# Hybrid stages: values products half a slot later, a preloaded mask under the decay rows, and wider Exp instructions

## The reference, cut to what matters

```
def hybrid_mixer(h, w_in, ...):
    proj = h @ w_in
    q, k, v, z, xbc, dt = split(proj)
    attn = dilated_attention(rotary(q), rotary(k), v)      # 8 heads of 64
    xbc = silu(causal_depthwise_conv(xbc)); xs, bm, cm = split(xbc)
    dt = softplus(dt + dt_bias)
    y = ssd_chunked(xs, dt, -exp(a_log), bm, cm) + d_skip * xs
    return concat([attn, groupnorm(y * silu(z))]) @ w_out
def segsum_exp(a):                                          # in ssd_chunked, per chunk of 128 and head (16)
    cs = cumsum(a)
    return exp(where(lower_triangle, cs[:, None] - cs[None, :], -inf))
```

## Time and profile before

| what | value |
|---|---|
| times of three runs | 2692.08, 2696.5, 2701.61 us; median 2696.5 |
| span of the profiled execution (first to last instruction) | 2693.9 us, the only time that the page gives for it |
| PE busy | 2601.8 us, 97% of the span |
| DVE, ACT, POOL busy | 1815.6 us (67%), 1467.9 us (54%), 173.1 us (6%) |
| chain that ended last, by engine | PE 83%, DVE 7%, ACT 5% |
| mean granted TensorE clock | 0.993 |

### The profile page before, as it was taken

How to read it: one execution, slowest core, us unless ns; L and a number is a source line. 1 busy time by engine, 2 the same in 40 slices (tenths; PEclk the granted TensorE clock), 3 DMA queues, 4 the chain that set the end, 5 groups by cost and what they waited for, 6 DMA issues and landing times.

```text
span 2693.9 us, 44003 instructions
## 1 busy us (share of the span) xinstructions
PE 2601.8 (97%) x15456; PEld 2255.8 (84%) x15456; DVE 1815.6 (67%) x2565; ACT 1467.9 (54%) x2363; POOL 173.1 (6%) x253
## 2 busy tenths in 40 slices
PE   7999998999999989999989999999999999998999
PEld 6888887888888868888888688888888888887887
DVE  5766668666766666676676666676657667666766
ACT  4645447455555564565555655555555555555654
POOL 0010001000000030000001200000110000002000
PEclk9999999999999999999999999999999999999999
DMA  4458744477566436666654266666446665653664
GB/s 150 145 164 231 210 129 142 156 226 212 172 193 190 133 121 208 191 184 193 187 176 153 70 199 191 177 192 191 141 149 183 196 202 168 192 157 121 180 189 146
DMA packets 581774, 465.44 MB, mean 173 GB/s; under 512 B 19524, under 2 KB 542372, under 8 KB 581156
## 3 DMA queue, kind: packets, MB, share of 16 engines
q1 hardware_dynamic: 579300, 456.10, 56.3%
q0 software_dynamic: 1632, 7.37, 1.1%
q10 hardware_dynamic: 736, 0.56, 0.1%
HBM read 460.76 MB, written 4.25 MB: 173 GB/s over the span
## 4 chain that ended last, share of the span: by engine, by line
PE 83%; DVE 7%; ACT 5%; issue 2%; DVEq 2%; DMA 1%; POOL 1%; SPq 0%; ACTq 0%; POOLq 0%
PE acc L783 19%; PE gu L750 14%; PE tp L750 13%; PE tp L757 7%; PE gu L757 7%; PE acc L816 3%; DVE lo_a L452 3%; ACT hi_a L440 1%; PE acc L1454 1%; PE acc L1456 1%; PE acc L1455 1%; PE gu L701 1%; PE gu L1412 1%; PE tp L1327 1%; PE gu L1413 1%
## 5 line engine op out<-in xcount | busy, mean ns | idle before, releaser
L452 DVE TENSOR_TENSOR lo_a<-raw_a,hi_a 128x2048 fp32r<-128x2048 f32 (+1 forms) x313 | 711.1, 2272 | 357.4 <-ACT hi_a L440 356.1
L440 ACT ACTIVATE hi_a<-raw_a 128x2048 fp32r<-128x2048 f32 (+1 forms) x313 | 591.5, 1890 | 119.0 <-PE acc L1456 27.4
L750 PE MATMUL tp<-xT,hi_a 128*128 128x512 f32 x1600 | 398.4, 391 | 0.0
L750 PE MATMUL gu<-xT,hi_a 128*128 128x512 f32 x1600 | 397.9, 391 | 0.0
L750 PEld LDWEIGHTS gu<-xT,hi_a 128*128 128x128 f32 x1600 | 294.0, 188 | 56.9
L750 PEld LDWEIGHTS tp<-xT,hi_a 128*128 128x128 f32 x1600 | 293.4, 188 | 56.4
L783 PE MATMUL acc<-hi_b,h_hi 128*128 128x512 f32 x760 | 298.6, 393 | 1.6 <-issue 1.1
L783 PE MATMUL acc<-lo_b,h_hi 128*128 128x512 f32 x760 | 298.0, 392 | 0.0
L783 PE MATMUL acc<-hi_b,h_lo 128*128 128x512 f32 x760 | 295.7, 389 | 0.0
L464 DVE TENSOR_TENSOR lo_b<-raw_b,hi_b 128x1024 fp32r<-128x1024 f32 x210 | 255.9, 1219 | 0.0
L842 ACT ACTIVATE arena<-arena 128x256 f32<-128x256 f32 x200 | 83.6, 418 | 282.0 <-DVE arena L905 282.0
(11 more groups left out here) (329 smaller groups left out, 4109.4 us busy)
## 6 DMA issues: line engine op xcount, KB each, us to landing
raw_a<-in_ffn_w_in SPq DMA_DIRECT2D x352, 512.0 KB, 5.7
raw_b<-in_ffn_w_out SPq DMA_DIRECT2D x176, 512.0 KB, 3.6
raw_a<-in_w_in SPq DMA_DIRECT2D x52, 512.0 KB, 4.7
raw_a<-in_w_gate SPq DMA_DIRECT2D x44, 512.0 KB, 5.5
raw_a<-in_w_up SPq DMA_DIRECT2D x44, 512.0 KB, 6.7
raw_b<-in_w_down SPq DMA_DIRECT2D x44, 512.0 KB, 4.4
raw_a<-in_w_out SPq DMA_DIRECT2D x24, 512.0 KB, 4.2
raw_a<-in_c_w_in SPq DMA_DIRECT2D x24, 512.0 KB, 4.5
```

The source lines that it names most:

```text
L440: nc.scalar.activation(a_view(hi_a, par)[:, :, 0:width], a_view(raw_a, par)[:, :, 0:width], ACT.Copy).then_inc(a_hi, 1)
L452: nc.vector.tensor_tensor(a_view(lo_a, par)[:, :, 0:width], a_view(raw_a, par)[:, :, 0:width], a_view(hi_a, par)[:, :, 0:width].bitcast(F3 ...
L750: nc.tensor.matmul(banks[:, e, :], w_hi[:, kt, e * P:(e + 1) * P], xT[:, :, kt, :], start=(kt == 0), stop=False)
```

## The change

1. Values products of the hybrids run four half slots after the scores (before: three), and write PSUM bank `acc[:, 2, 0:256]` (before: a part of `tp`). The transposes no longer wait for `o_lo`; the values products do instead, that of unit 0 for `cs_out`. ScalarE's copy comes at the end of its half slot, after the hi split; VectorE's part half a slot after that.
2. At `p` = 11 VectorE runs `softplus_sum_dve` before the lo split (before: after it).
3. The triangular mask is loaded by two SP DMAs of 1 MB each into `mTs` ahead of slot 4's load (`masks_sync`); GpSimd's DMA adds the decay rows onto it (`accum_op`), in one run of 8 KB per partition (before: 512 B). VectorE adds the per-partition values (`segments_dve`, `p` = 15 and 17) in place of the mask. ScalarE runs Exp over eight heads at a time without bias, four instructions (before: 32), at `p` = 17 and 19.
4. ScalarE preloads, at `p` = 9, a table set that has both Exp and Ln.
5. `bc_pe` waits for `o_lo` of unit 3 in place of `cs_out`.

```diff
@@ mixer_sync
+                if s.kind == "hybrid" and i == 4:
+                    masks_sync(sp, s)
                 if n >= 2:
                     sp.wait_ge(a_lo, n - 1)
...
+        def masks_sync(sp, s):
+            if s.k == 0:
+                sp.wait_ge(bias_row_ready, 1)
+            else:
+                for t in range(NT):
+                    sp.wait_ge(x_ready[t], 2 * s.k)
+            lo, hi = CC["negtri"]
+            for c in range(NT):
+                sp.dma_start(mTs[c], T["constants"][:, lo:hi].unsqueeze(1).broadcast_to([P, SSM_HEADS, P])).then_inc(mask_in, 16)
@@ decay_pool
+            pool.wait_ge(mask_in, 32 * (L + 1))
             for c in range(NT):
-                pool.dma_start(mTs[c], decay_rows[L, c].partition_broadcast(P)).then_inc(row_in[c], 16)
+                src = decay_rows[L, c].rearrange("h l -> (h l)").partition_broadcast(P)
+                pool.dma_start(mTs[c].rearrange("p h l -> p (h l)"), src, accum_op=ALU.add).then_inc(row_in[c], 16)
@@ woven_turn_pe
-            elif w >= 1:
+            elif w >= 1 and s.kind != "hybrid":
                 pe.wait_ge(o_lo, s.pair0 + w)
@@ woven_values_pe
             pe.wait_ge(pt_act, g + 1)
+            if s.kind == "hybrid":
+                pe.wait_ge(*((o_lo, s.pair0 + w) if w else (cs_out, s.layer + 1)))
@@ middle_pe
-            if scored(s, p - 3) is not None and s.kind != "B":
-                woven_values_pe(pe, s, scored(s, p - 3))
+            behind = p - (4 if s.kind == "hybrid" else 3)
+            if scored(s, behind) is not None and s.kind != "B":
+                woven_values_pe(pe, s, scored(s, behind))
@@ bc_pe
-            pe.wait_ge(cs_out, L + 1)
...
+            pe.wait_ge(o_lo, s.pair0 + 4)
@@ hybrid_act
                     if p == 9:
+                        nc.scalar.preload_act_table_set("natural_log_exp_and_others")
                         narrow_evac_act(act, s, 3, dt_out)
...
-                    if scored(s, p - 3) is not None:
-                        values_act(act, s, scored(s, p - 3))
...
-                    if 15 <= p < 19:
-                        decay_act(act, s, (p - 15) // 2, 2 * ((p - 15) % 2))
+                    if p in (17, 19):
+                        decay_act(act, s, (p - 17) // 2)
...
                     if h == 0:
                         ahead_a(hi_slot_a, act, s.a0 + i + 1)
+                    if scored(s, p - 4) is not None:
+                        values_act(act, s, scored(s, p - 4))
@@ decay_act
+            for g in range(SSM_GROUPS):
+                m = mTs[c][:, 8 * g:8 * g + 8, :]
+                nc.scalar.activation(m, m, ACT.Exp).then_inc(seg_exp, 1)
@@ hybrid_dve
+                    if p == 11:
+                        softplus_sum_dve(dve, s)
                     if h == 1:
                         ahead_a(lo_slot_a, dve, s.a0 + i + 1)
...
-                    if scored(s, p - 3) is not None:
-                        values_dve(dve, s, scored(s, p - 3))
+                    if scored(s, p - 5) is not None:
+                        values_dve(dve, s, scored(s, p - 5))
...
-                    if p in (14, 16):
-                        causal_dve(dve, s, (p - 14) // 2)
+                    if p in (15, 17):
+                        segments_dve(dve, s, (p - 15) // 2)
@@ segments_dve (was causal_dve)
-            nc.vector.tensor_tensor(mTs[c], mTs[c], C("negtri").unsqueeze(1).broadcast_to([P, SSM_HEADS, P]), ALU.add)\
+            nc.vector.tensor_tensor(mTs[c], mTs[c], ncs[:, 16 * c:16 * c + 16].unsqueeze(2).broadcast_to([P, SSM_HEADS, P]), ALU.add)\
```

More of the change, by code:

```diff
@@ L359, in build_block @@
         row_in = [sem("row_in0"), sem("row_in1")]
+        mask_in = sem("mask_in")
         cs_ps, cs_out, decays, xdec_ready = sem("cs_ps"), sem("cs_out"), sem("decays"), sem("xdec_ready")
@@ L1255, in build_block, with values_bank @@
         turn_flat = tp[:, :, :].rearrange("p b c -> p (b c)")[:, 0:768]
+        def values_bank(s):
+            return acc[:, 2, 0:256] if s.kind == "hybrid" else tp[:, 1, 256:512]
         def score_banks(s, w):
@@ L1326, in woven_values_pe @@
                         cols_t = slice(512 + hh * P, 512 + (hh + 1) * P) if t else slice(hh * 256, (hh + 1) * 256)
-                        mm = nc.tensor.matmul(tp[r, 1, 256 + t * P:512], v[:, t, c:c + HD], probs_t[:, cols_t],
+                        mm = nc.tensor.matmul(values_bank(s)[r, t * P:256], v[:, t, c:c + HD], probs_t[:, cols_t],
                                               start=(j == pair[0] and t == 0), stop=(t == 1 and s.kind != "B"))
@@ L1506, in values_act @@
             act.wait_ge(o_ready, s.pair0 + u + 1)
-            nc.scalar.activation(oT_hi[:, u, :], tp[:, 1, 256:512], ACT.Copy).then_inc(o_hi, 1)
+            nc.scalar.activation(oT_hi[:, u, :], values_bank(s), ACT.Copy).then_inc(o_hi, 1)
         def exp_act(act, s, w):
@@ L1548, in values_dve @@
             dve.wait_ge(o_hi, s.pair0 + u + 1)
-            nc.vector.tensor_tensor(oT_lo[:, u, :], tp[:, 1, 256:512], oT_hi[:, u, :].bitcast(F32),
+            nc.vector.tensor_tensor(oT_lo[:, u, :], values_bank(s), oT_hi[:, u, :].bitcast(F32),
                                     ALU.subtract).then_inc(o_lo, 1)
@@ L2108, in silu_act, with decay_act @@
             nc.scalar.activation(conv[:, 2 * r:2 * r + 2, :], conv[:, 2 * r:2 * r + 2, :], ACT.Silu).then_inc(silued, 1)
[L2110 to L2116, removed]
+        def decay_act(act, s, c):
+            act.wait_ge(seg_ready, 2 * s.layer + c + 1)
+            for g in range(SSM_GROUPS):
+                m = mTs[c][:, 8 * g:8 * g + 8, :]
+                nc.scalar.activation(m, m, ACT.Exp).then_inc(seg_exp, 1)
         def square_y_act(act, s, c):
@@ L2155, in hybrid_dve @@
                         nc.vector.tensor_tensor(csd, ncs[:, 0:16], ncs[:, 32:48], ALU.subtract).then_inc(cs_out, 1)
-                    if p in (10, 11):
-                        (softplus_ratio_dve, softplus_sum_dve)[p - 10](dve, s)
+                    if p == 10:
+                        softplus_ratio_dve(dve, s)
                     if scored(s, p - 1) is not None:
@@ L2289, in softplus_sum_dve, with segments_dve @@
                                            ALU.mult, ALU.mult).then_inc(dt_done, 1)
-        def causal_dve(dve, s, c):
+        def segments_dve(dve, s, c):
             dve.wait_ge(row_in[c], 16 * (s.layer + 1))
-            nc.vector.tensor_tensor(mTs[c], mTs[c], C("negtri").unsqueeze(1).broadcast_to([P, SSM_HEADS, P]), ALU.add)\
+            nc.vector.tensor_tensor(mTs[c], mTs[c], ncs[:, 16 * c:16 * c + 16].unsqueeze(2).broadcast_to([P, SSM_HEADS, P]), ALU.add)\
                 .then_inc(seg_ready, 1)
@@ L2299, in mask_dve @@
             for g in range(SSM_GROUPS):
-                dve.wait_ge(seg_exp, 8 * s.layer + 4 * c + 2 * g + 2)
+                dve.wait_ge(seg_exp, 4 * s.layer + 2 * c + g + 1)
                 m = mTs[c][:, 8 * g:8 * g + 8, :]
```

## The result

The changed kernel takes 2704.15 us (median of 18 runs, 2700.22 to 2707.78), the kernel before 2696.47 in 18 runs. The ratio is 1.0022, 95% interval 1.0016 to 1.0029: slower by some 6 us (7.7 by the medians), less than the 0.3% that I had called the limit, though with so many runs it can be told from none. The profiled execution took 2702.33 us, its span is 2700.5 against 2693.9.

The account below looks back on a forecast made before the run. VectorE's chain was taken as the bound, ScalarE second. First hybrid 3.8 - 1.3 = +2.5 us, second -1.3, so +1.2 on the span 2693.9, plus 2.6 from span to median: 2698 us; range 2688 to 2707.

Parts of the forecast that it names:

- no change of over 0.3%: Whole kernel: the time changes by under 0.3%, 8 us, which can't be told from none; chance 0.69.
- Masks, first hybrid: SP's queue ahead of slot 4: mask loads make its lo split 3.8 us late, bounds 1.0 to 9.6.
- rival 1: First hybrid: masks take over 10 us, VectorE 9.6 us late, TensorE then at low clock; 2705 us; chance 0.15.
- Masks, second hybrid: SP's queue behind slot 3's loads: masks cost nothing, cover 3 us; at 6.6 us per mask, 5 us late.
- Softplus ahead of the lo split: VectorE at `p` = 11: sums end 2.4 us earlier; TensorE's two waits of 1.9 and 2.0 us become one of 3.
- a rival, 1.7 us each: Hybrids: stalls merge, one more low-clock stretch costs up to 1.7 us per hybrid; 2701 us; chance 0.07 in full.
- Values half a slot later: Hybrids: unit 2's maxima 2.7 us earlier; TensorE stalls of 1.5, 1.5 and 2.3 us replace two copy waits.
- Decays: Hybrids: ScalarE's Exps 5.6 us less work, VectorE's work unchanged; last taps 1.3 us earlier, the gain per hybrid.
- Table set: ScalarE: two table loads of 1.28 us become one, three become one in the second hybrid; nothing on the path.
- Added rows: GpSimd's adding DMAs of decay rows: no cost; both chunks may take 25 us in all before anything moves.
- Rival 2: Hybrids: all 12.5 us of TensorE's listed waits vanish, with low-clock stretches; 2684 us, half 2690; chance 0.16 in full or half.

Follow-up runs that it names:

- masks_behind5: The changed kernel with the mask DMAs issued behind slot 5's weights instead of ahead of slot 4's; 2697.07 us, 0.9997 of the kernel before.
- best_b: values_undone with the first chunk's row sums added behind the taps of `p` = 16 and three Silus behind slot 10's tap; 2687.35 us, 0.9958 of the kernel before.
- values_undone: masks_behind5 with the whole values edit taken back, so values products run three half slots after the scores; 2688.54 us, 0.9966 of the kernel before.
- late_two_areas: masks_behind5 with the hybrids' values products alternating between two PSUM banks; 2694.96 us, 0.9994 of the kernel before.

## Why the prediction held, and where it did not

The time, the range and "no change of over 0.3%" held, in part by luck: three terms were mis-sized, and two of them, of opposite sign, nearly cancel. Without the masks' place the hybrids lose 1.5 us in masks_behind5 where I had forecast a gain of 2.6; the masks add 6.9 in the first hybrid where I had forecast 3.8.

- *Masks, first hybrid.* Forecast 3.8 us, bounds 1.0 to 9.6; slot 4 was 7.6 late, and their place cost 7.1 us of time (2704.15 against 2697.07). The step that failed is "at the 380 KB per us of weight loads": the masks moved at 216 to 290 and were in place 10.4 us after issue, where the forecast has 6.6 (1.1 and 5.5), and 2.1 us of SP's time went for issuing them. Slot 4's split followed 3.6 us later, as I had taken it with completion. The low clock behind TensorE's wait of 7.2 us, which I had given to rival 1 alone, came too. This is rival 1's mechanism by its own sign (two masks took over 10 us) and nearly its time, 2705.
- *Masks, second hybrid.* Hidden, as forecast; the cover of 3 us was just used up.
- *Softplus ahead of the lo split.* "2.4 us earlier" was right as an interval, but I priced it into one number of 1.3 us per hybrid with the rest. Alone it is worth 7.8 us by the medians and 5.3 in the two hybrids; the trace puts that to the loss of a stall and of low-clock stretches that followed, but how much is stall and how much clock was not separated. I had weighed those only as a rival, 1.7 us each, and read them as a cost that might be added, not as one that the kernel before already pays twice in its first hybrid.
- *Values half a slot later.* Forecast as a gain, "2.7 us won"; it loses: 6.1 us alone and 8.5 behind softplus first by the medians, 5.2 and 9.2 in the two hybrids. I had written the reason down myself ("the two waits of 1.9 and 2.0 us become one of 3 us"; 2.6 to 2.8 measured, 5.0 alone, and 1.1 only behind the changed kernel's late slot 4) and then counted it as no loss. The product that waited for ScalarE was also what TensorE did while VectorE worked on the sums. That the stall grew is shown; whether the later product or the later copies that go with it make it grow was not tried apart. The new waits for `oT_lo` came as forecast, 3.6 us in three, each up to 1.3.
- *Decays.* Two Exps took 2.00 us, 1.00 each, as forecast from the earlier trace rows (1.04). The last taps did not win by it: VectorE still waits 2.35 us ahead of them, 1.60 in the earlier trace rows. VectorE's operation was priced at 2.29; the first of a hybrid's two takes 2.62, and GpSimd beside it 3.66 instead of 1.61, a cost that I had not seen.
- *Table set.* The loads fell from two to one and from three to one, as forecast; no run has this edit alone, so that it costs nothing is not shown.
- *Added rows.* No loss in time in the changed kernel, as taken; in best_b, where the rest is quicker, they are the next bound, by the weights behind them and not by VectorE's wait, which was the one way I had looked for. They landed 10.6 us after issue (median of four), plain ones in 5.9. The rule of the Trainium skill quoted there ("Collectives: The Full Stack", section "The bandwidth ceiling: the fold count and why AG ≠ RS ≠ AR"), half the rate of a copy, is near to this ratio of 1.8; weight loads moved beside the adding rows, so it is no clean test.
- *Rival 2* ("the waits go in full", 2684) is close to what values_undone and best_b show, but by another way: the values products stay, and the sums come first. The clock does not stay up everywhere: best_b still has 0.83 from 90 to 100 us.

The gain of a hybrid is not always kept. In best_b the drift is -10.15 us at 878 us and -8.61 at 963, in a stage that no edit touches; the changed kernel lost 1.4 there. The kernel before, best_b and the changed kernel have the same single wait of TensorE there, 1.8 us for VectorE's `x`. What differs is the clock behind it; the kernel before and best_b at the same work:

```profile
910.00:920.00 10.00, 10.00 (x88) 10.00 (x88) 7.35 (x10) 4.12 (x6) 1.57 (x4) 1.00 0.29 95
```

```profile
900.00:910.00 10.00, 10.00 (x82) 10.00 (x81) 7.09 (x10) 3.96 (x6) 1.57 (x4) 0.92 0.31 98
```

The changed kernel has 0.93 there, values_undone and late_two_areas 1.00, and neither lost anything at this place. So after one and the same stall the clock fell in some executions and not in others, about 1.4 us a time. What decides it stays open. For the readings above it means that a stretch at the low clock in one trace is in part luck; the times, medians of 5 to 18 runs, and what an edit does to a stall, seen in both hybrids, carry the argument.

## What to carry to other kernels

A wait in a list is not a cost until it is known what the engine would do in its place: work that waits for one engine may be the filler of a wait for another, and moving it merges two short stalls into one, behind which the clock can drop. Look which stretches at the low clock the kernel already pays, and ask of each edit whether it splits or merges the stall ahead of them; but take the price from several runs, since the same stall need not be followed by the same clock. A load put into a queue costs the bytes ahead of whatever stands behind it there; put it behind the load that is next needed.

## What the hardware showed that was not expected

- After TensorE's stall of 7.2 us the granted clock stood at 0.50 from 52 to 60 us and reached 1.00 only at about 62, though TensorE was busy without a gap from 56 on. After a wait of 1.8 us it was 0.90 to 0.93 in some executions (the changed kernel, best_b) and 1.00 in others (the kernel before, values_undone).
- Two DMAs that read the same 512 bytes 16 times per partition took SP 2.09 us to issue and moved at 290 KB per us from 44 to 48 us; in 8 KB pieces of another matrix as many bytes took 0.82 us to issue and moved at 355. The issue time is not of the pieces alone: behind the loads of slots 4 and 5 the first two took SP 5.11 us.
- A GpSimd product beside a 128x2048 VectorE operation with a broadcast operand ran 3.66 us instead of 1.61 (two products), and the VectorE operation 2.62 instead of 2.29; moved apart, 1.62 and 2.29. The Trainium skill, "SBUF — State Buffer", section "🔬 SBUF: two separate sides", has VectorE and GpSimd share a pair of ports that one instruction holds to its end, also where VectorE reads two inputs from SBUF; the 2.05 us that the product grew are near to the length of that operation, and agree.
- 1 MB DMAs that add onto what is in place landed in 10.6 us (median), plain ones in 5.9; in values_undone the DMA engines' share was 0.97 to 1.07 from 75 to 85 us at only 193 to 225 KB per us.
